# Six raw weight slots for the expert loop, two of them over the scan's rows, and gates as (tanh(x/2) + 1) / 2

## The chip, the cores and the metric

The kernel runs on one core of a Trainium2 chip (trn2). The metric is the device time of one execution in microseconds; the time before is 1294.22 us, the median of three runs (1288.75 to 1295.73). The engines are named as in the profile: PE is TensorE, DVE VectorE, ACT ScalarE, POOL GpSimd and SP SyncE, whose queue issues most of the weight loads.

## What is computed

Two layers of a backbone run over 128 context tokens and 128 latent tokens of width 1024, with one set of weights. Cut to what matters:

```python
# per layer, for each of the two streams
out = token_mixer(x * (1 + sc1) + sh1)
x = layer_norm(ALPHA * x + g1 * out)
ff = hier_moe(x * (1 + sc2) + sh2)
x = layer_norm(ALPHA * x + g2 * ff)

# token_mixer: three branches, then gates and one projection
gates = sigmoid(proj[..., OFF_GATE:N_IN].reshape(b, l, 3, D_MODEL))
merged = (gates[:, :, 0] * (y_att @ w_branch[0])
          + gates[:, :, 1] * (y_ssm @ w_branch[1])     # scan in two directions
          + gates[:, :, 2] * (y_gm @ w_branch[2]))
return merged @ w_o, k, v, h_fin

# hier_moe: 4 groups of 8 experts; a token takes one group and 2 of its experts
hid = silu(einsum('td,edf->tef', x, w1)) * einsum('td,edf->tef', x, w3)
y = einsum('tef,efd->td', hid * gates[:, :, None], w2)
```

## The kernel before

All weights are fp32. Each passes the core as a *piece* of 128 partitions by 2048 columns (1 MB) in four steps: a load into a slot of `raw`; ACT copies it into `wh` as fp32r, the high part; DVE subtracts the high part from the raw piece and gets the low part `wl`; PE multiplies with three products (high by high, high by low, low by high). There are 4 slots (`SLOTS`) and 3 pairs of parts (`PARTS`). A slot is free for the next load when DVE has subtracted (`part_low`), a pair of parts when PE has used both (`part_free`).

The mixer's pieces of a layer are listed in `PIECES`, those of the MoE in `BODY`: three for each of 32 experts, up (first half of the rows of w1 and w3), up (second half), and down. Every token is gathered by group, so an expert works on 128 rows. PE's order in the loop (`stream`) is: up of expert i, down of expert i - 1, transposition of the hidden rows of expert i. ACT takes the Silu (line 1772) between its conversions (line 1721), DVE the product with the gate (`hid`, line 2488) between its subtractions (line 1816, a helper for all its two-operand work). In the first group DVE also finishes the layer norm (experts 2 to 5, `x<-x,lnrow`). For each group but the first, POOL gathers the group's rows from memory (line 909, tile `grow`), and PE transposes them within experts 4 and 6 of the group before. After a group PE scatters its sum.

SyncE's queue takes the loads in their fixed order (`load`, line 732; `expert_loads`, lines 747 and 750). The first four pieces of a loop wait for the slots of the last mixer pieces, the last of which is the router's. Piece 4 waits for DVE's subtraction of piece 0, which follows the routing. Before piece 4 the queue also waits for the routing's decision, whether one round of the loop is enough (`need_ready`); it is, in these runs.

In the mixer, the scan of the state space branch runs in eight steps. In step n DVE forms the exponents `seg` (line 2291), ACT takes Exp of them (line 1692), for n of 4 and more also of the decay rows, `eb` (line 1689), DVE forms `W` (line 2313), and PE uses it in four small matmuls. Between the steps PE projects the gates of branches 2 and 1 (`SCAN_FILL`), one piece a step; ACT and DVE convert the pieces ahead. ACT evaluates the gates (`gate_take`, line 1605) after steps 2, 4 and 6 and after the last one, and before the scan for branch 0, just behind the Gelu of `gv`. `merge` multiplies them with the projected branches and adds; the merged rows are transposed and cut into high and low parts (`mT`, line 1708), and the output projection follows. Exp and Sigmoid alternate in the scan, and so do their tables, which ACT loads with ACT_TABLE_LOAD.

## Time and profile before

| | |
|---|---|
| median of 3 runs | 1294.22 us (1288.75 to 1295.73) |
| the profiled execution | 1292.93 us, of which the span of the profile is 1291.1 |
| PE busy | 1215.4 us, 94% of the span |
| DVE busy | 970.8 us, 75% |
| ACT busy | 740.6 us, 57% |
| POOL busy | 74.5 us, 6% |
| DMA | 358.83 MB, mean 278 GB/s |
| mean clock granted to PE | 0.966 |
| MoE loops, first to last Silu | 360.65 to 645.47 and 984.29 to 1266.54 us |
| scans, layer 0 and 1 | about 225 to 285 and 853 to 913 us |

Times in the views are microseconds from the span's start. A row of the timeline or of the groups names line, engine and operation, then output <- inputs with their shapes; behind it in brackets stands the idle time just before and the instruction that ended it. Busy time of PE counts matmuls that overlap in its pipeline, so a busy PE isn't at its peak. The clock is a share of full speed.

### The profile page before, as it was taken

Reading aid. Unit: us, or ns where it says so; the run is one execution under the profiler, and the core shown is the slowest. Engines: PE = TensorE matmul, PEld = TensorE weight load, DVE = VectorE, ACT = ScalarE, POOL = GpSimd, SP = SyncE. Lnnn points to the kernel's source line nnn. Section 1 sums busy time; section 2 is a strip of 40 time slices with the busy share of each in tenths; the row PEclk is TensorE's granted clock in tenths of the full one; section 3 lists DMA queues with packets and bytes.
Section 4 is the critical chain, followed back from the end, with each engine's and each line's share of the span. In section 5 each row is a group of like instructions: output and inputs, shape, how many; then the busy total and the mean of one; then the engine's idle time right before and its main releaser. Section 6 shows DMA issues by size and latency. Waiting matters only on the chain.

```text
span 1291.1 us, 15762 instructions
## 1 busy us (share of the span) xinstructions
PE 1215.4 (94%) x5950; PEld 950.3 (74%) x5953; DVE 970.8 (75%) x1159; ACT 740.6 (57%) x700; POOL 74.5 (6%) x121
## 2 busy tenths in 40 slices
PE   5999999999999999999979999998998999999994
PEld 1667777777677788887857777877777778788883
DVE  1645657787589889888878375768968988988887
ACT  1543553753467677677753255546437776777773
POOL 0401000101000000000020000010000000000000
PEclk8899998989999999999999999988999999999997
DMA  9978864636879999999976777445347999999991
GB/s 355 301 269 305 301 209 140 192 112 260 331 272 355 378 361 340 354 353 348 364 213 234 274 256 273 164 138 184 135 164 256 362 373 352 353 345 364 349 357 65
DMA packets 99491, 358.83 MB, mean 278 GB/s; under 512 B 9188, under 2 KB 12736, under 8 KB 83024
## 3 DMA queue, kind: packets, MB, share of 16 engines
q1 hardware_dynamic: 87504, 295.12, 63.2%
q0 software_dynamic: 11904, 62.63, 14.1%
q8 instruction: 49, 0.80, 0.2%
q14 instruction: 34, 0.28, 0.1%
HBM read 352.92 MB, written 5.83 MB: 278 GB/s over the span
## 4 chain that ended last, share of the span: by engine, by line
PE 65%; DVE 15%; DMA 8%; ACT 6%; issue 3%; DVEq 2%; ACTq 1%; SPq 1%; POOL 0%; POOLq 0%
PE bank L940 61%; DVE wl L1816 7%; DMA raw<-in_moe_w 5%; PE bank L943 4%; ACT wh L1721 2%; ACT wh L1511 2%; DMA first<-in_w_ada 1%; DMA adaw<-in_w_ada 1%; DVE tmp L1816 1%; DMA decay<-decay_rows 1%; DVE seg L2291 1%; ACTq L1606 0%; DVE xbc L2085 0%; DVE xbc L2082 0%; DVE x L1816 0%
## 5 line engine op out<-in xcount | busy, mean ns | idle before, releaser
L1816 DVE TENSOR_TENSOR wl<-raw,wh 128x2048 fp32r<-128x2048 f32 (+1 forms) x268 | 607.6, 2275 | 126.7 <-ACT wh L1511 67.0
L1721 ACT ACTIVATE wh<-raw 128x2048 fp32r<-128x2048 f32 x192 | 367.7, 1916 | 63.8 <-PE bank L940 28.4
L940 PE MATMUL bank<-wh,xgh 128*128 128x512 f32 x512 | 210.1, 410 | 0.0
L940 PE MATMUL bank<-wh,xgl 128*128 128x512 f32 x512 | 203.6, 398 | 0.0
L1511 ACT ACTIVATE wh<-raw 128x2048 fp32r<-128x2048 f32 (+1 forms) x76 | 142.3, 1872 | 100.2 <-PE bank L940 57.5
L940 PE MATMUL bank<-wh,hTh 128*128 128x512 f32 x448 | 186.2, 416 | 4.4 <-DVE wl L1816 2.5
L940 PE MATMUL bank<-wl,hTh 128*128 128x512 f32 x448 | 182.4, 407 | 0.0
L940 PE MATMUL bank<-wh,hTl 128*128 128x512 f32 x448 | 181.8, 406 | 0.0
L940 PE MATMUL bank<-wl,xgh 128*128 128x512 f32 x512 | 140.3, 395 | 0.0
L940 PEld LDWEIGHTS bank<-wl,xgh 128*128 128x128 f32 x512 | 96.1, 188 | 23.5 <-DVE wl L1816 0.2
L940 PEld LDWEIGHTS bank<-wh,xgl 128*128 128x128 f32 x512 | 97.1, 190 | 20.2
L940 PEld LDWEIGHTS bank<-wh,xgh 128*128 128x128 f32 x512 | 97.4, 190 | 19.6
L940 PEld LDWEIGHTS bank<-wh,hTh 128*128 128x128 f32 x448 | 87.8, 196 | 27.9 <-DVE wl L1816 4.9
L940 PEld LDWEIGHTS bank<-wh,hTl 128*128 128x128 f32 x448 | 87.3, 195 | 21.5
L940 PEld LDWEIGHTS bank<-wl,hTh 128*128 128x128 f32 x448 | 87.5, 195 | 19.5
L940 PE MATMUL bank<-wh,hTTh 128*128 128x512 f32 x256 | 101.3, 396 | 0.0
L940 PE MATMUL bank<-wh,hTTl 128*128 128x512 f32 x256 | 101.2, 395 | 0.0
L940 PE MATMUL bank<-wl,hTTh 128*128 128x512 f32 x256 | 80.7, 396 | 0.5 <-DVE wl L1816 0.4
L1778 ACT ACTIVATE hTTh<-bank 128x256 fp32r<-128x256 f32 x64 | 24.6, 384 | 66.5 <-PE bank L943 63.8
L940 PEld LDWEIGHTS bank<-wl,hTTh 128*128 128x128 f32 x256 | 47.9, 188 | 12.9 <-DVE wl L1816 1.4
L940 PEld LDWEIGHTS bank<-wh,hTTh 128*128 128x128 f32 x256 | 48.1, 188 | 11.8 <-issue 0.3
L940 PEld LDWEIGHTS bank<-wh,hTTl 128*128 128x128 f32 x256 | 48.1, 188 | 11.5
(303 smaller groups left out, 1480.1 us busy)
## 6 DMA issues: line engine op xcount, KB each, us to landing
raw<-in_moe_w SPq DMA_DIRECT2D x256, 512.0 KB, 5.2
raw<-in_moe_w SPq DMA_DIRECT2D x64, 1024.0 KB, 7.2
raw<-in_w_in SPq DMA_DIRECT2D x52, 1024.0 KB, 5.6
adaw<-in_w_ada POOLq DMA_DIRECT2D x32, 1024.0 KB, 5.7
raw<-in_w_branch SPq DMA_DIRECT2D x12, 1024.0 KB, 5.3
raw<-in_w_ada SPq DMA_DIRECT2D x8, 1024.0 KB, 9.9
raw<-in_w_o SPq DMA_DIRECT2D x8, 1024.0 KB, 4.9
first<-in_w_ada SPq DMA_DIRECT2D x4, 1024.0 KB, 16.7
```

The costliest lines, as they stand in the source:

```text
L940: return behind(nc.tensor.matmul(*args, **kw))
L943: return behind(nc.tensor.transpose(*args))
L1511: A_(wh[c][:, 0:n], raw[:, r, 0:n], ACT.Copy).then_inc(part_high[c], 1)
L1721: tally(A_(wh[c][:, :], raw[:, r, :], ACT.Copy), part_high[c])
L1778: tally(A_(hTTh[i == NE - 1][:, :, :], bank[TURN_BANK][:, 0:FF].rearrange("p (c t) -> p c t", c=2), ACT.Copy), hidT_high)
L1816: return V.tensor_tensor(o, a, b, op)
L2291: ins = V.tensor_scalar(seg[:, n % 2, i, :], decay[n % 2][:, i, :], acs[:, s, 8 * r + h:8 * r + h + 1], 0.0, ALU.subtract, ALU.min)
```

## The change

**The ring.** The expert loop takes its raw pieces from six slots instead of four. Slots 4 and 5 lie in a region `scan_rows` of 21 KB a partition, which holds in the mixer `rows3`, `wsT`, `h0`, `h0T`, `xbc` and `btok`; these are dead once the scan's branch is done and the new state is stored. So the first use of slot 4 in each layer waits for `y_ready[1]` and for `stored`. A piece of the loop now waits for the piece six before it, and at the loop's end the next layer's first four pieces wait for pieces 90 to 93 instead of 92 to 95. Conversion and subtraction find their slot modulo `RING`. The number of part pairs stays 3.

**The gates.** sigmoid(x) = (tanh(x/2) + 1) / 2. ACT evaluates Tanh with a scale of 0.5; the product in `merge` becomes (t + 1) * branch in one instruction; the factor 1/2 is applied where the merged rows are read from the transposition, on ACT as the scale of the copy and on DVE inside the subtraction.

The diff, with the renumbering of semaphore counts left out:

```diff
@@ -38,6 +38,7 @@
 SLOTS = 4
+RING = 6
 PIECE = 2048
@@ -92,15 +93,15 @@
-def slot_count(pieces, k):
-
-    return sum(incs(pieces[i]) for i in range(k % SLOTS, k + 1, SLOTS))
-
-
-LOAD_A = [[slot_count(p, k) for k in range(len(p))] for p in PIECES]
-LOAD_B = [slot_count(BODY, k) for k in range(len(BODY))]
-FULL_A = [a[-SLOTS:] for a in LOAD_A]
-FULL_B = LOAD_B[-SLOTS:]
+def slot_count(pieces, k, slots):
+
+    return sum(incs(pieces[i]) for i in range(k % slots, k + 1, slots))
+
+
+LOAD_A = [[slot_count(p, k, SLOTS) for k in range(len(p))] for p in PIECES]
+LOAD_B = [slot_count(BODY, k, RING) for k in range(len(BODY))]
+FULL_A = [a[-SLOTS:] + [0] * (RING - SLOTS) for a in LOAD_A]
+FULL_B = LOAD_B[-RING:]
 RAW_AT = [[p.index(key) for key in SPLIT] for p in PIECES]
@@ -364,13 +365,6 @@
         hrow = sb("hrow", [P, 40])
-        rows3 = sb("rows3", [P, 3, NW])
-        wsT = sb("wsT", [P, 4, P])
-        h0 = sb("h0", [HD, 2, HEADS, HD])
-        stout = h0
-        h0T = sb("h0T", [P, HEADS, HD])
-        xbc = sb("xbc", [P, 6, 2 * P])
-        btok = sb("btok", [P, 2 * P])
         tmp = sb("tmp", [P, D])
@@ -401,6 +395,18 @@
             return [nc.alloc_sbuf_tensor_at(n, shape, dt, offset=start + o * 1024) for n, shape, dt, o in tensors]
+
+        rows3, wsT, h0, h0T, xbc, btok, raw4, raw5 = region(
+            "scan_rows", 21,
+            ("rows3", [P, 3, NW], F32, 0),
+            ("wsT", [P, 4, P], F32, 6),
+            ("h0", [HD, 2, HEADS, HD], F32, 8),
+            ("h0T", [P, HEADS, HD], F32, 12),
+            ("xbc", [P, 6, 2 * P], F32, 14),
+            ("btok", [P, 2 * P], F32, 20),
+            ("raw4", [P, PIECE], F32, 0), ("raw5", [P, PIECE], F32, 8))
+        stout = h0
+        slot = [raw[:, i, :] for i in range(SLOTS)] + [raw4[:, :], raw5[:, :]]
@@ -734,20 +740,24 @@
                     kind, e, *h = BODY[i]
-                    s = i % SLOTS
-                    if i >= SLOTS:
-                        body_emptied(l, rnd, i - SLOTS)
+                    s = i % RING
+                    if i >= RING:
+                        body_emptied(l, rnd, i - RING)
                     elif rnd:
-                        body_emptied(l, 0, len(BODY) - SLOTS + i)
-                    else:
+                        body_emptied(l, 0, len(BODY) - RING + i)
+                    elif i < SLOTS:
                         slot_emptied(l, len(PIECES[l]) - SLOTS + i)
+                    elif i == SLOTS:
+                        sp.wait_ge(y_ready[1], l + 1)
+                        sp.sem_inc(sp_waited, 1)
+                        sp.wait_ge(stored, 48 * (l + 1))
                     if kind == "up":
...
                             src = A[w][l, e].rearrange("(p c) f -> p (c f)", c=DC)
-                            sp.dma_start(raw[:, s, n * 1024:(n + 1) * 1024],
+                            sp.dma_start(slot[s][:, n * 1024:(n + 1) * 1024],
                                          src[:, h[0] * 1024:(h[0] + 1) * 1024]).then_inc(slot_full[s], 16)
                     else:
-                        sp.dma_start(raw[:, s, :], A["moe_w2"][l, e].rearrange("(p c) n -> p (c n)", c=2)).then_inc(slot_full[s], 16)
+                        sp.dma_start(slot[s], A["moe_w2"][l, e].rearrange("(p c) n -> p (c n)", c=2)).then_inc(slot_full[s], 16)
@@ -765,22 +775,22 @@
                     load(l, i)
-                expert_loads(l, 0, 0, SLOTS)
+                expert_loads(l, 0, 0, RING)
                 sp.wait_ge(need_ready, l + 1)
...
                 with sp.If(more < 1):
-                    expert_loads(l, 0, SLOTS, len(BODY))
-                    for i in range(SLOTS):
-                        body_emptied(l, 0, len(BODY) - SLOTS + i)
+                    expert_loads(l, 0, RING, len(BODY))
+                    for i in range(RING):
+                        body_emptied(l, 0, len(BODY) - RING + i)
                         sp.sem_inc(slot_full[i], FULL_B[i])
-                        if l < L - 1:
+                        if l < L - 1 and i < SLOTS:
                             load(l + 1, i)
                 with sp.Else():
-                    expert_loads(l, 0, SLOTS, len(BODY))
+                    expert_loads(l, 0, RING, len(BODY))
                     expert_loads(l, 1, 0, len(BODY))
                     for i in range(SLOTS if l < L - 1 else 0):
-                        body_emptied(l, 1, len(BODY) - SLOTS + i)
+                        body_emptied(l, 1, len(BODY) - RING + i)
                         load(l + 1, i)
@@ -1602,7 +1612,7 @@
                         t = bank_full(act, l, name)
-                        frees(A_(dst[:, s, n * 512:(n + 1) * 512], t[:, :], ACT.Sigmoid), name)
+                        frees(A_(dst[:, s, n * 512:(n + 1) * 512], t[:, :], ACT.Tanh, scale=0.5), name)
                         act.drain().then_inc(gate_ready, 1)
@@ -1706,7 +1716,7 @@
                         A_(hTh[:, 4 * h:4 * h + 4, s * P:(s + 1) * P], t[:, :].rearrange("p (c t) -> p c t", c=4),
-                           ACT.Copy).then_inc(turned_high, 1)
+                           ACT.Copy, scale=0.5).then_inc(turned_high, 1)
                 ahead(("wo", 3))
@@ -1715,10 +1725,10 @@
                 def convert(tally, rnd, j):
-                    r, c = j % SLOTS, j % PARTS
+                    r, c = j % RING, j % PARTS
                     act.wait_ge(slot_full[r], N_LOAD[r].moe(l, rnd, LOAD_B[j]))
                     act.wait_ge(part_free[c], N_PART[c].moe(l, rnd, j // PARTS + 1))
-                    tally(A_(wh[c][:, :], raw[:, r, :], ACT.Copy), part_high[c])
+                    tally(A_(wh[c][:, :], slot[r], ACT.Copy), part_high[c])
@@ -1918,11 +1928,14 @@
-                def turned(b, name, high, low):
-
-                    t = bank[USE[l][name][0]]
+                def turned(b, name, high, low, scale=None):
+
+                    t = bank[USE[l][name][0]][:, :].rearrange("p (c t) -> p c t", c=4)
                     dve.wait_ge(turned_high, l * 10 + b + 1)
-                    frees(tt(low, t[:, :].rearrange("p (c t) -> p c t", c=4), high.bitcast(F32), ALU.subtract), name)
+                    if scale is None:
+                        frees(tt(low, t, high.bitcast(F32), ALU.subtract), name)
+                    else:
+                        frees(V.scalar_tensor_tensor(out=low, in0=t, scalar=scale, in1=high.bitcast(F32), op0=ALU.mult, op1=ALU.subtract), name)
@@ -2145,19 +2158,23 @@
                     gates_ = gate1 if b == 1 else gate
+
+                    def gated(out, t, s, hs):
+                        return V.scalar_tensor_tensor(out=out, in0=gates_[:, s, hs], scalar=1.0, in1=t[:, :], op0=ALU.add, op1=ALU.mult)
+
                     for h in range(2):
...
                                 t = bank_full(dve, l, f"br{b}{h}{s}")
-                                frees(tt(tmp[:, s * 512:(s + 1) * 512], t[:, :], gates_[:, s, hs], ALU.mult), f"br{b}{h}{s}")
+                                frees(gated(tmp[:, s * 512:(s + 1) * 512], t, s, hs), f"br{b}{h}{s}")
                                 drain()
...
                             out = merged[:, s, hs] if b == 0 else tmp[:, s * 512:(s + 1) * 512]
-                            frees(tt(out, t[:, :], gates_[:, s, hs], ALU.mult), f"br{b}{h}{s}")
+                            frees(gated(out, t, s, hs), f"br{b}{h}{s}")
                         if b:
@@ -2336,12 +2353,12 @@
                         part = (slice(None), slice(4 * h, 4 * h + 4), slice(s * P, (s + 1) * P))
-                        turned(6 + 2 * s + h, f"mT{s}{h}", hTh[part], hTl[part])
+                        turned(6 + 2 * s + h, f"mT{s}{h}", hTh[part], hTl[part], 0.5)
                 ahead(("wo", 3))
                 def lower(tally, rnd, j):
-                    r, c = j % SLOTS, j % PARTS
+                    r, c = j % RING, j % PARTS
                     dve.wait_ge(part_high[c], N_PART[c].moe(l, rnd, j // PARTS + 1))
-                    tally(tt(wl[c][:, :], raw[:, r, :], wh[c][:, :].bitcast(F32), ALU.subtract), part_low[c])
+                    tally(tt(wl[c][:, :], slot[r], wh[c][:, :].bitcast(F32), ALU.subtract), part_low[c])
...
                 rows("x2T", 1)
```

## Rows read from the trace of the kernel before

**Rows 1.** Table of stretches, one group of eight experts each: us, busy time of each engine, PE clock, DMA share, GB/s
```profile
370.88:445.41 74.53, 72.15 (x319) 56.85 (x318) 69.10 (x56) 52.68 (x44) 1.61 (x2) 1.00 0.97 363
...
518.29:591.74 73.45, 73.05 (x327) 58.72 (x326) 63.45 (x48) 52.68 (x45) 0.96 (x1) 1.00 0.95 349
...
992.24:1067.34 75.10, 72.25 (x319) 56.85 (x318) 69.53 (x56) 53.03 (x45) 1.60 (x2) 1.00 0.98 365
...
1140.30:1212.81 72.51, 72.51 (x327) 58.92 (x326) 63.71 (x48) 52.55 (x45) 0.97 (x1) 1.00 0.97 356
```

**Rows 2.** Timeline of ACT, line 1772 in layer 0: start, length, idle before
```profile
591.74 0.39 ACT L1772 ACTIVATE sil<-bank 128x256 f32<-128x256 f32 x1 [0.16 <-PE bank L940]
602.22 0.39 ACT L1772 ACTIVATE sil<-bank 128x256 f32<-128x256 f32 x1 [0.59 <-PE bank L940]
610.86 0.39 ACT L1772 ACTIVATE sil<-bank 128x256 f32<-128x256 f32 x1 [0.59 <-PE bank L940]
```

**Rows 3.** Waits, 345:680, then 950:1291: total us, times, longest
```profile
ACT wh L1721 <- DMA raw<-in_moe_w: 15.6, 21, 2.5
```
```profile
ACT wh L1721 <- DMA raw<-in_moe_w: 10.4, 12, 2.0
```

**Rows 4.** Chain of work in layer 0's loop: start, us, what
```profile
382.73 8.51 DMA raw<-in_moe_w
391.26 1.93 ACT wh L1721
393.21 2.29 DVE wl L1816
```

**Rows 5.** Timeline of PE in the scan, last step of layer 0, step 4 of layer 1
```profile
278.35 0.69 PE L940 MATMUL bank<-xs,W 128*128 128x64 f32 x2 [2.08 <-DVE W L1816]
```
```profile
888.80 0.56 PE L940 MATMUL bank<-xs,W 128*128 128x64 f32 x2 [3.06 <-DVE W L1816]
```

**Rows 6.** Timeline of SyncE's queue, then table of stretches, at the loops' start
```profile
351.44 0.33 SPq L750 DMA_DIRECT2D raw<-in_moe_w  x1
```
```profile
350.00:370.00 20.00, 18.73 (x93) 16.29 (x93) 15.48 (x40) 11.64 (x12) 0.00 (x0) 0.84 0.65 239
...
980.00:990.00 10.00, 8.73 (x43) 7.02 (x42) 7.49 (x20) 7.02 (x7) 0.00 (x0) 1.00 0.39 136
```

**Rows 7.** Timelines of ACT and of DVE at expert 1 of layer 0
```profile
370.88 0.39 ACT L1772 ACTIVATE sil<-bank 128x256 f32<-128x256 f32 x1 [0.59 <-PE bank L940]
```
```profile
373.98 0.48 DVE L2488 SCALAR_TENSOR_TENSOR hid<-bank,gg,sil 128x256 f32<-128x256 f32 x1
```

**Rows 8.** Groups of instructions on ACT: count, busy us, mean ns, idle before
```profile
L1605 ACT ACT_TABLE_LOAD x10 | 12.8, 1283 | 0.2
```

**Rows 9.** Chain of work in the scans of layer 0 and layer 1
```profile
249.98 1.30 ACTq L1606
...
252.75 1.28 ACT L1689
```
```profile
869.83 1.28 ACT L1692
...
882.45 1.28 ACT L1689
```

**Rows 10.** Table of stretches, end of the scan of layer 0
```profile
280.00:285.00 5.00, 5.00 (x14) 3.99 (x14) 4.00 (x9) 1.52 (x3) 0.00 (x0) 0.53 0.19 77
```

**Rows 11.** Groups of instructions on DVE, 350:680, by line
```profile
L2488 DVE SCALAR_TENSOR_TENSOR hid<-bank,gg,sil 128x256 f32<-128x256 f32 x32 | 15.3, 478 | 0.4
L1816 DVE TENSOR_TENSOR hTTl<-bank,hTTh 128x256 fp32r<-128x256 f32 x32 | 13.4, 418 | 3.0 <-ACT hTTh L1778 3.0
```

**Rows 12.** The tile grow, then timelines of GpSimd and PE
```profile
DMA to landing us min/median/max: 6.4/7.5/8.0
```
```profile
383.32 1.01 POOL L909 DMA_INDIRECT grow<-token_rows,slot_row  x1 [34.27 <-DVE slot_row L2466]
```
```profile
395.90 0.66 PE L943 MATMUL bank<-cst,grow 128*128 128x128 f32 x4
```

More of the change, by code:

```diff
@@ L86 @@
     assert len(_p) % SLOTS == 0 and [p for p in _p if p[0] not in RAW_KINDS] == SPLIT
-assert len(BODY) % SLOTS == 0 and len(BODY) % PARTS == 0
+assert len(BODY) % RING == 0 and len(BODY) % PARTS == 0
 ROUNDS = 2
@@ L121, in moe @@
         return self.base[l] + self.a[l] + rnd * self.b + n
-N_LOAD = [Loop([FULL_A[l][i] for l in range(L)], FULL_B[i]) for i in range(SLOTS)]
+N_LOAD = [Loop([FULL_A[l][i] for l in range(L)], FULL_B[i]) for i in range(RING)]
 RAW_FREED = [[sum(p[i][0] in RAW_KINDS for i in range(k % SLOTS, k + 1, SLOTS)) for k in range(len(p))] for p in PIECES]
@@ L477, in hybrid_backbone @@
             at += n
-        slot_full = [sem(f"slot_full{i}") for i in range(SLOTS)]
+        slot_full = [sem(f"slot_full{i}") for i in range(RING)]
         slot_free = [sem(f"slot_free{i}") for i in range(SLOTS)]
```

## The prediction

> **What bounds the kernel now.** I read the table of stretches first, cut at the starts of one group of experts, because TensorE (PE) is busy 94% of the span and an average hides where it waits. An undisturbed group of eight experts takes 72.51 us, the last of [rows 1]. [rows 2] give the beat inside it: 8.64 us from expert to expert, and 10.48 where a scatter lies between, so a scatter costs 1.84. The first group of a layer has no scatter and should take 72.51 - 1.84 = 70.67 us. It takes 74.53 and 75.10 in [rows 1], which is 3.86 and 4.43 too long, and the third group of layer 0 is 0.94 too long. I take the rest of the MoE loops as PE at its own pace.
>
> The waits name the cause of part of this: ScalarE (ACT) waits 15.6 and 10.4 us for raw weights in the two loops [rows 3]. In the chain of work [rows 4] one turn of a slot is visible: 8.51 us for the load, 1.93 to convert, 2.29 to subtract, after which the slot takes its next load. That is 12.7 us, over 4 slots 3.2 us a piece or 9.5 us an expert, more than the 8.64 that PE needs. The loop's start is bound by the latency of a ring too short. It isn't bound by it alone: the group moves 363 GB/s at a DMA share of 0.97 and VectorE (DVE) is busy 69.10 of its 74.53 us [rows 1].
>
> The second place is the scan of the mixer. There the chain runs through ACT and DVE, and PE waits for the matrix W before its small matmuls: 3.06 us in layer 1 and 2.08 us at the last step in layer 0 [rows 5].
>
> **The ring: what is moved.** Two more slots add no transfer; pieces 4 and 5 of each loop are issued earlier. In the old order piece 4 waits for the first subtraction and is issued at 351.44 [rows 6]. In the new one SyncE's queue issues slots 4 and 5 right behind slot 3. The two waits put ahead of slot 4 (the branch rows ready, the state stored) concern work of the scan, over some 50 us earlier, so nothing behind them in the queue, the wait for the routing's decision among it, is held up. Is there room on the DMA engines? In 350 to 370 us their share is 0.65 and in 980 to 990 it is 0.39 [rows 6], so 7.0 and 6.1 us of a full set of engines lie idle. Two pieces are 2.10 MB; at the 363 GB/s of [rows 1] they take 5.8 us and fit. The loop thus starts its steady part with 5.8 us of lead, and each later load is issued two turns earlier, which takes the 12.7 us turn to 12.7 / 6 = 2.1 us a piece. The latency is gone as a limit.
>
> What is late next? DVE. [rows 7] show expert 1 of layer 0: its first product is read at 370.88, and DVE, which has run without a gap, only writes the hidden rows from 373.98 to 374.46. PE fills the time with one down projection (12 of the 36 matmuls of an 8.64 us beat, 2.9 us), so it waits some 0.7 us, and a little more through the refill behind it. This doesn't depend on the ring. The lower bound of what stays in a first group is this 0.7 us; the upper one is the DVE time itself: 69.10 us busy and about 2.5 of gaps, 71.6 to 73 us for the group. I take 71.9, 1.2 above PE's own pace, nearer the first end because the DVE row already contains that stall. The first groups then give 74.53 - 71.9 = 2.6 and 75.10 - 71.9 = 3.2 us, and the third of layer 0 its 0.94: **6.7 us**. The shorter first group must draw part of its 27 MB (363 x 74.53) from the lead, 2.6 us x 363 GB/s = 0.9 MB of the 2.1, so the lead suffices. Bounds: 3 us (DVE keeps the first groups at 73 and above) and 9.2 (all of 3.86 + 4.43 + 0.94). The first loads of the next layer go out two pieces earlier too; PE has its own work there, so I give them 0, and less than 0.5 either way.
>
> **The gates: what is removed.** Tanh stands in for Sigmoid at line 1605. [rows 8]: a table load is 1283 ns and ten of them precede a gate. All ten go if Tanh is in the tables that Exp and Gelu use, and with them the reloads for Exp behind the gates in the scan; the ten alone are 12.8 us of ACT, but most of it lies beside PE's work. What counts is the loads on the chain [rows 9]. In layer 0 there is one pair, 249.98 and 252.75, 2.58 us together, just ahead of the exponential that DVE waits for; the pair of gate (2,0) there is covered, since PE runs on without a gap until W of step 4. In layer 1 the first W is later and the chain holds two pairs, the reloads at 869.83 and 882.45 and as many loads ahead of the gates, 5.1 us. The two exponentials and gates between them stay.
>
> What follows behind these is DVE's own chain, busy almost throughout, so it shifts by what ACT gives. In layer 0 the last W matmul stands at 278.35 and moves by 2.5; the lower bound is 2.1 (no more than PE's own wait there goes), the other 3.7, if the earlier ACT work also lets DVE run ahead before step 4 (half of the pair that was covered). In layer 1 the shift is at most 5.1. PE, however, runs at 0.53 of its clock in 280 to 285 after its waits at the end of layer 0's scan [rows 10], the lower of the two levels (1.2 of 2.4 GHz). After the change the W of the last two steps is what PE waits for in layer 1 too, so part of the gain can be given back there. I take 4.0 for layer 1, between 2.5 and 5.1. **The scan gives 6.5 us**, bounds 4.6 and 8.8. The Trainium skill ("ScalarE: Activation LUTs", "Table sets: the hidden batching unit") puts tanh into the set of exp, and sigmoid into another; by that rule the reloads of the scan vanish. The same page ("What ACT_TABLE_LOAD costs") adds a drain of 1380 ns to each switch, by which three pairs would be 16 us; the trace disagrees, as the chain gives the switch at 249.98 1.30 us in all, and the sum keeps that.
>
> The other edits: the gate product becomes a scalar_tensor_tensor on DVE (24 times), the four subtractions of a layer behind the merge too, and the copy of ACT gets a factor. The nearest rows are the 256-column pair of the loop [rows 11], 478 ns against 418. At 60 ns each, 32 operations are 1.9 us at most, nearly all beside matmuls, and some in the DVE chain ahead of the output projection. I take 0.3 us lost, between 0 and 1.9.
>
> **Sum.** 6.7 + 6.5 - 0.3 = 12.9 us. The profiled execution took 1292.93 us (span 1291.1 and 1.8 around it), so it would become 1280.0. It stands 1.3 us below the median 1294.22 of the runs shown, and so the median becomes **1281.3 us**.
>
> **Rivals.** (a) *The clock takes it back.* A stretch like 280 to 285 at 0.53 of the clock loses 5 x 0.47 = 2.4 us. If PE's new waits bring one more such stretch in each layer, 4.8 us go: 1286. For it: W of steps 6 and 7 comes out 1 to 3 us after PE wants it. Against it: the stretch may lie where PE has slack anyway, and layer 0 has one already. (b) *The loop stays bound by DVE and bandwidth.* The first groups keep 74 us or more; the ring gives 1 us and the scan 6.5: 1287. For it: DVE at 93% and DMA at 0.97. Against: 26.0 us of ACT waits for loads [rows 3] that DVE doesn't explain. (c) *Tanh doesn't share the tables*, the switches stay: the ring alone, 1287.5. (d) *More than forecast*: DVE gets ahead in both places, 9.2 + 8.8 = 18.0: 1276. (e) *Slower: the gathers.* The deeper ring keeps more raw loads in flight while GpSimd gathers the rows of the next group. [rows 12]: a gather issued at 383.32 lands 7.5 us later, at 390.8, and PE turns its rows at 395.90, 5.1 us of slack. Two more pieces served ahead would make it 13.3 us, only 0.7 us of wait, six times over: 4 us, not enough. To end 0.5% slower the six gathers must eat 12.9 + 6.5 = 19.4 us, 3.2 each, so they must land after 5.1 + 3.2 + 7.5 = 15.8 us: 1301. It decides only from twice the present time. The Trainium skill ("DMA: Bandwidth & Descriptors", "Queues, rings and completion order") has each DMA engine take turns between queues packet by packet, by which a gather in GpSimd's queue isn't behind SyncE's loads at all; no row here shows it.
>
> **Chances and range.** Forecast 0.62, (a) 0.12, (b) 0.12, (c) 0.05, (d) 0.06, (e) 0.03. About 0.5% (6.5 us) is what this measurement can tell from no change. Faster by more: the forecast, (d), nearly all of (a), two thirds of (b): 0.86. Within 0.5%: 0.11. Slower: 0.03. The range goes from the case (d) with the 3 us by which single runs of before differ, 1273, to (b) and (c) with 1.5 us above, 1289.
>
> **What would show it.** Right: no table load at 1605, 1689 or 1692; W waits of PE shifted from step 4 to steps 6 and 7; first groups near 72 us; ACT's wait for raw loads in the loops below 5 us. The ring is wrong if the first groups stay at 74 us with these waits gone (DVE or bandwidth), or if the waits stay. The gates are wrong if the step from the first W matmul to the last stays as long. A gather that lands after 13 us, or half clock in 860 to 920, would break the sum.

## The result and the profile after

| | before | after |
|---|---|---|
| median | 1293.09 us (1288.75 to 1298.76, 7 runs) | 1278.48 us (1276.04 to 1283.68, 7 runs) |
| ratio | | 0.9905 (0.9881 to 0.993), 9 to 15 us |
| the profiled execution | 1292.93 us, span 1291.1 | 1282.84 us, span 1281.0 |
| ACT instructions | 700 | 684 |
| loops, first to last Silu | 284.82 and 282.25 us | 281.19 and 279.14 us |

The change is faster, by about 1%, and the median lies 2.8 us below the forecast of 1281.3. The profiled execution is one of the slower of the kernel after. I split the 10.1 us between the two profiles by milestones: the first `W` matmul of a scan, the first one of its last step (called the last W below), and the first and the last Silu of a loop, each read in the timelines of PE and ACT:

| stretch, us | before | after | difference |
|---|---|---|---|
| start to first W, layer 0 | 232.33 | 234.81 | +2.5 |
| first to last W, layer 0 | 46.02 | 43.20 | -2.8 |
| last W to first Silu | 82.30 | 79.32 | -3.0 |
| loop, layer 0 | 284.82 | 281.19 | -3.6 |
| last Silu to first W, layer 1 | 214.39 | 213.71 | -0.7 |
| first to last W, layer 1 | 48.20 | 44.36 | -3.8 |
| last W to first Silu | 76.23 | 80.74 | +4.5 |
| loop, layer 1 | 282.25 | 279.14 | -3.1 |
| last Silu to the end | 24.56 | 24.53 | 0 |

The scans and the loops are where the change acts: 6.6 and 6.7 us. The rest moves by itself, up to 4.5 us in one stretch, and has to be told apart from it.

The table of stretches after, as in [rows 1] (us, busy time of PE, weight loads, DVE, ACT and GpSimd, PE clock, DMA share, GB/s): the first group of experts of each layer, the second of layer 0, the end of the scan and the loop's start as in [rows 10] and [rows 6], and the routing of layer 1.

```profile
366.12:439.76 73.64, 71.49 (x319) 57.02 (x318) 70.36 (x57) 52.44 (x45) 1.61 (x2) 1.00 0.99 375
985.27:1057.68 72.41, 71.46 (x319) 56.97 (x318) 69.27 (x56) 52.44 (x44) 1.59 (x2) 1.00 1.00 383
439.76:512.27 72.51, 72.51 (x327) 58.92 (x326) 64.19 (x51) 52.43 (x44) 0.99 (x1) 1.00 0.97 355
280.00:285.00 5.00, 4.78 (x21) 3.52 (x19) 4.26 (x9) 0.20 (x1) 0.00 (x0) 1.00 0.14 56
350.00:370.00 20.00, 16.51 (x82) 13.24 (x81) 16.61 (x35) 12.39 (x11) 0.00 (x0) 1.00 0.92 346
960.00:965.00 5.00, 3.95 (x20) 3.86 (x18) 1.76 (x11) 4.04 (x6) 0.71 (x1) 0.50 0.94 303
965.00:970.00 5.00, 4.14 (x19) 4.17 (x20) 3.90 (x11) 1.60 (x3) 0.00 (x0) 0.50 0.98 364
```

All groups but the first are at 72.51 to 72.54 us. The idle DMA time at the loop's start is used: a share of 0.92 where [rows 6] had 0.65. Half clock stood at the end of layer 0's scan before [rows 10] and isn't there now; it stands at the routing of layer 1 instead.

The waits after, in both loops. ACT's wait for raw weights [rows 3] is in neither list; what is left there is DVE waiting for the conversion:

```profile
DVE wl L1826 <- ACT wh L1731: 23.7, 51, 1.4
```

PE's waits for W, as in [rows 5]: steps 6 and 7 of layer 0, steps 4, 6 and 7 of layer 1.

```profile
273.84 0.43 PE L950 MATMUL bank<-xs,W 128*128 128x64 f32 x2 [1.68 <-DVE W L1826]
278.01 0.43 PE L950 MATMUL bank<-xs,W 128*128 128x64 f32 x2 [2.08 <-DVE W L1826]
877.32 0.41 PE L950 MATMUL bank<-xs,W 128*128 128x64 f32 x2 [0.51 <-DVE W L1826]
892.42 0.43 PE L950 MATMUL bank<-xs,W 128*128 128x64 f32 x2 [1.86 <-DVE W L1826]
896.59 0.43 PE L950 MATMUL bank<-xs,W 128*128 128x64 f32 x2 [2.07 <-DVE W L1826]
```

The wait of 3.06 us at step 4 of layer 1 has become 0.51. Step 4 of layer 0 has no wait any more; before, it had this one, which [rows 5] don't show:

```profile
259.09 0.41 PE L940 MATMUL bank<-xs,W 128*128 128x64 f32 x2 [2.40 <-DVE W L1816]
```

The chain in the scan no longer runs through ACT: there is no table load at the gates [rows 8] nor at the two exponentials.

Expert 1 of layer 0, as in [rows 7]: first PE, then DVE.

```profile
368.61 0.74 PE L950 MATMUL bank<-wl,hTTh 128*128 128x512 f32 x2 [1.59 <-DVE wl L1826]
371.29 0.48 PE L953 MATMUL bank<-cst,hid 128*128 128x128 f32 x2 [0.56 <-DVE hid L2505]
```
```profile
366.26 4.49 DVE L1826 TENSOR_TENSOR wl<-raw,wh 128x2048 fp32r<-128x2048 f32 x2
370.67 0.48 DVE L2505 SCALAR_TENSOR_TENSOR hid<-bank,gg,sil 128x256 f32<-128x256 f32 x1
```

DVE is busy without a gap from 359.34 to 373.68, and PE waits 2.15 us for it, at a low part and at the hidden rows.

### The profile page after: what moved, and what is told of

It is laid out like the page before. It is cut to its first block, busy times and chain, and to the rows that moved or that the text cites. A ratio compares the mean times of both kernels' runs of the same rounds, so it can differ in the third digit from the quotient of the medians.

```text
span 1281.0 us, 15755 instructions
## 1 busy us (share of the span) xinstructions
PE 1208.1 (94%) x5953; PEld 949.2 (74%) x5953; DVE 971.0 (76%) x1159; ACT 716.9 (56%) x684; POOL 74.5 (6%) x121
## 3 DMA queue, kind: packets, MB, share of 16 engines
q0 software_dynamic: 11904, 62.63, 13.9%
## 4 chain that ended last, share of the span: by engine, by line
PE 73%; DVE 11%; DMA 5%; ACT 4%; issue 2%; DVEq 2%; ACTq 1%; SPq 1%; POOL 0%; POOLq 0%
PE bank L950 69%; PE bank L953 4%; DVE wl L1826 4%; ACT wh L1521 2%; DMA adaw<-in_w_ada 2%; DMA first<-in_w_ada 1%; DMA raw<-in_w_in 1%; DVE tmp L1826 1%; DVE seg L2308 1%; DVEq L2333 1%; DMA decay<-decay_rows 1%; DVE xbc L2098 0%; DVE xbc L2095 0%; SPq L763 0%; DVE gv L1826 0%
## 5 line engine op out<-in xcount | busy, mean ns | idle before, releaser
L950 PEld LDWEIGHTS bank<-wh,xgh 128*128 128x128 f32 x512 | 96.8, 189 | 20.2 <-DVE xgl L1826 0.8
L950 PEld LDWEIGHTS bank<-wh,xgl 128*128 128x128 f32 x512 | 96.5, 189 | 20.2
```

What stands on the lines that cost most here:

```text
L950: return behind(nc.tensor.matmul(*args, **kw))
```

## The experiments

The milestones in the texts below are read as in the table above.

### The gates alone

The kernel before with all edits of the gates, and four slots in the loop:

```diff
-                        frees(A_(dst[:, s, n * 512:(n + 1) * 512], t[:, :], ACT.Sigmoid), name)
+                        frees(A_(dst[:, s, n * 512:(n + 1) * 512], t[:, :], ACT.Tanh, scale=0.5), name)
```

> The gates alone, with four slots in the loop as before. My theory (the gates' table loads stand on the chain of the scan, the ring acts on the loop alone): 5 to 7 us faster than before; no table load at the gate or at the two exponentials; from the first scan matmul to the last W matmul 2.5 to 3 us less in layer 0 and 4 to 4.5 us less in layer 1; the W waits of step 4 gone and steps 6 and 7 at 1.7 to 2.1 us; the first groups of experts unchanged at 74.5 and 75.1 us with ScalarE's waits for raw weights between 10 and 16 us a loop. Rival, that the whole gain comes from the ring: within 1 us of before. Rival, that the clock at the end of the scan eats it: 2 to 3 us faster.

Measured: ratio 0.9943 (0.9913 to 0.9972) over 9 runs, 7.4 us faster, between 3.6 and 11.2. From the first to the last W 43.35 us in layer 0 and 44.09 in layer 1, that is 2.7 and 4.1 less than before. Both rivals fall. One expectation missed: the loops aren't unchanged but longer, 286.79 and 283.59 us, and the first groups took 77.63 and 76.85. ACT's waits for raw weights are there as expected, 12.4 and 12.9 us. The first group of layer 0, and a stretch within it:

```profile
364.65:442.28 77.63, 73.90 (x319) 57.98 (x318) 69.09 (x56) 52.76 (x44) 1.61 (x2) 0.98 0.94 351
420.00:425.00 5.00, 3.59 (x15) 2.27 (x13) 3.78 (x2) 3.42 (x3) 0.00 (x0) 1.00 1.02 410
425.00:430.00 5.00, 4.00 (x12) 3.25 (x13) 5.00 (x8) 2.86 (x3) 0.00 (x0) 0.66 0.98 347
```

In 420 to 425 the DMA engines are full and 410 GB/s arrive, yet each engine stands for a part of the time: ACT waits 1.60 us for a raw piece at 421.22, DVE 1.22 for ACT, and PE 1.86 for DVE's hidden rows at 426.00. In 425 to 430 the granted clock is 0.66. No profile with six slots has a wait of ACT for raw weights in its list; that four slots can't bridge such a stall is my reading of that.

### The ring alone

The kernel after with all edits of the gates taken back:

```diff
-                        frees(A_(dst[:, s, n * 512:(n + 1) * 512], t[:, :], ACT.Tanh, scale=0.5), name)
+                        frees(A_(dst[:, s, n * 512:(n + 1) * 512], t[:, :], ACT.Sigmoid), name)
```

> The ring of six slots alone, with Sigmoid and its table loads. My theory: 6 to 7 us faster than before (3.6 in the first loop, 3.1 in the second, and little elsewhere); the first groups near 73.6 and 72.4 us, all others at 72.5; no wait of ScalarE for raw weights in the loops; the scan as before. Rival, that DVE and not latency holds the loop's start: under 2 us faster, first groups at 74 or more. Together with the gates alone it should give the whole change, 12 to 14 us, if the two parts are independent.

Measured: ratio 0.9955 (0.9933 to 0.9977) over 12 runs, 5.8 us faster, between 3.0 and 8.7. The loops are 281.16 and 279.17 us, as after the whole change; the scans take 46.09 and 48.07 us, as before (PE waits 2.47 us for W at step 4 of layer 0). 7.4 and 5.8 make 13.2, the change 12.3 by its ratio: within their intervals the two parts add up.

### The kernel before once more

No edit.

> The kernel before once more, for a second profile. The kernel with the gates alone had loops of experts 2.0 and 1.3 us longer than the profiled execution of before, with the same four slots. If a ring of four slots makes the loops vary from execution to execution with the service of the loads, this one's loops differ from 284.8 and 282.3 us by 0.5 us or more, while with six slots every profile shows 281.2 and 279.1 within 0.1. If the gates themselves slow the loops, it shows 284.8 and 282.3 again.

Measured: 1292.39 us in one run; loops of 284.78 and 281.40, first groups of 75.31 and 74.51 (74.53 and 75.10 in [rows 1]). So with four slots the three profiles give for both loops together 567.1, 566.2 and 570.4 us, and with six the profiles of the change, the ring alone, the next kernel and the one with 64 bytes further down give 560.0 to 560.3. With six slots the gates don't slow the loops. With four it is less clear: the two profiles of the kernel before agree in the loop of layer 0 (284.82 and 284.78) and differ by 0.85 us in that of layer 1, where I had put the mark at 0.5, and the 570.4 us stand in one profile, the only one with the gates. That four slots lose another amount in each execution fits this; that the gates add to it there isn't excluded.

### Six slots without the lead

```diff
                         sp.wait_ge(stored, 48 * (l + 1))
+                    if not rnd and SLOTS <= i < RING:
+                        body_emptied(l, 0, i - SLOTS)
```

> The whole change, but the first loads of slots 4 and 5 wait for the subtractions of pieces 0 and 1, so that the loop has six slots without the lead of two pieces. If the latency of a slot's turn is what held the first groups, this keeps most of the gain: at most 1 us slower than the change, first groups at 73 to 74. If it is the lead that gives the gain (the loads are bound by bandwidth and the two pieces fill idle time of the DMA engines), the first groups return to 74.5 and 75 and it is 3 to 6 us slower than the change.

Measured: 1278.55 us, ratio 0.989 (0.9861 to 0.9919), the same as the change. Its first groups:

```profile
362.58:436.22 73.64, 71.50 (x319) 57.04 (x318) 70.36 (x57) 52.44 (x45) 1.61 (x2) 1.00 0.99 377
979.31:1051.71 72.40, 71.45 (x320) 57.29 (x320) 69.26 (x56) 52.45 (x45) 1.60 (x2) 1.00 0.99 384
```

Within 0.01 us the groups of the change. The early issue of pieces 4 and 5 isn't needed. But the run takes away less than its name says. In layer 0 pieces 4 and 5 are issued 14.3 and 13.9 us ahead of the first Silu after the change, and 8.3 and 3.9 us ahead of it here; pieces 6 and 7 wait for slots that are free by then, and follow at once. The 20 us that correspond to 350 to 370 after the change are these, with the DMA engines as busy as there:

```profile
346.47:366.47 20.00, 16.52 (x82) 13.25 (x81) 16.60 (x35) 12.40 (x11) 0.00 (x0) 1.00 0.93 329
```

So six slots fill the idle DMA time with or without the head start. Whether the loop needs the two more turns in flight or the transfers in that idle time, no run separates.

### One pair of table loads put back

The kernel after, with one activation on a spare tile, behind the gate of step 4 and, in a second kernel, of step 2:

```diff
+        probe = sb("probe", [P, 2])
...
                         gate_take(*((2, 0), (2, 1), (1, 0))[n // 2 - 1])
+                    if n == 4:
+                        A_(probe[:, 0:1], C["iota"][:, 0:1], ACT.Sigmoid)
```

> The change with one activation of two columns more (a Sigmoid on a spare tile) on ScalarE behind the gate of step 4, in both layers; it brings back exactly the pair of table loads that stood on the chain before. Theory (the pair costs what its two loads take, 2.57 us plus some 0.2 for the activation, less what PE's cover hides): a W wait of 2 to 2.7 us at step 4 in layer 0 where there is none, in layer 1 the wait there grows from 0.5 to some 3 us, and the last W matmul, counted from the first, comes 2.5 to 2.8 us later in each layer. Rival, that a switch also drains the engine and costs as much again: 5 us or more. Rival, that the gain in the scan had another cause: under 1 us.

> The same added pair of table loads, but behind the gate of step 2. Theory: in layer 0 PE has cover there (it reaches W of step 2 to 4 without a wait), so the last W matmul moves by less than 1 us; in layer 1, where the gate projections run further ahead of DVE by the row of step 4 (0.5 us of wait), it moves by 1.5 to 2.8 us. Rival, that every pair costs its 2.6 us wherever it stands: 2.5 or more in both layers.

ACT in the first kernel, layer 0, then PE at step 4 in both layers of the first kernel:

```profile
251.07 1.28 ACT L1710 ACT_TABLE_LOAD   x1
252.36 0.20 ACT L1710 ACTIVATE probe<-cst 128x1 f32<-128x1 f32 x1
252.57 1.28 ACT L1700 ACT_TABLE_LOAD   x1
```
```profile
258.90 0.41 PE L951 MATMUL bank<-xs,W 128*128 128x64 f32 x2 [1.87 <-DVE W L1829]
876.98 0.41 PE L951 MATMUL bank<-xs,W 128*128 128x64 f32 x2 [3.16 <-DVE W L1829]
```

The two kernels took 1275.22 and 1269.50 us, one run each. They must be set against a kernel with the same placement of the tiles (the one with 32 bytes, below, 1265.11 us). From the first W to that of step 4 it needs 24.21 and 25.13 us; the pair at step 4 makes this 25.82 and 28.03, at step 2 24.58 and 26.42. A pair of 2.76 us with its activation costs 1.6 and 2.9 us at step 4, 0.4 and 1.3 at step 2. A load is 1.28 us and no more (251.07 + 1.28 = 252.35, and the probe starts at 252.36), so the rival with a drain falls, and so does the one that every pair costs its full length. Layer 0 has more cover at step 4 than I had expected (2.5 to 2.8 us), and layer 1 a little more at step 2 (1.5 to 2.8). The four prices add up to 6.2 us; the scans gave 6.6. By layer they fit less well: 2.0 us where layer 0 gave 2.8, and 4.2 where layer 1 gave 3.8. The pairs at step 6 and behind the last step weren't put back.

### What holds the scan after the change

```diff
-                    if n == 6:
-                        scanned(0)
                 branch_turned(2)
+                scanned(0)
...
-                branch_rows(l, 1, z)
-                branch(l, 2, (1,))
+                branch(l, 2, (1,), lambda: branch_rows(l, 1, z))
```

The function given to `branch` is called behind its first stream.

> The change, and behind it one more: VectorE takes the finishing of the first stream's scan rows (five operations, 3.8 us, between steps 6 and 7) after the last W, and TensorE turns the branch rows between the two streams of the last branch 2 piece instead of ahead of it. My theory: after the change the scan is bound by VectorE's chain in steps 5 to 7, not by ScalarE; the waits of 1.7 and 2.1 us for W at steps 6 and 7 go in both layers and some 1.4 us of a wait for z come back, so 2 to 3 us a layer, 4 to 6 us faster than the change. Rival: VectorE's total is the bound, the wait only moves to the turning of z or to the merge, and it is within 1 us of the change.

Measured: 1276.9 us, ratio 0.9878 (0.9853 to 0.9903); 3.5 us less than the change by the ratios and 1.6 by the medians, but the intervals overlap, so a gain isn't shown. The profile tells what happened. The waits for W at steps 6 and 7 are gone, from 3.76 to nothing in layer 0 and from 3.93 to 0.31 in layer 1, and these stand in layer 0 instead (in layer 1 the wait for z is 1.95 us):

```profile
283.19 1.23 PE L953 MATMUL bank<-cst,z 128*128 128x128 f32 x8 [1.78 <-DVE z L2345]
294.23 0.51 PE L950 MATMUL bank<-wh,yTh 128*128 128x512 f32 x1 [1.12 <-DVE wl L1827]
```

So both theories held in part: the order made the waits for W, and behind it the wait moves to z, by DVE's total. The 4 to 6 us of my theory aren't shown. The next kernel shortens it, and takes DVE off the loop's second expert:

```diff
-                    tt(y.rearrange("t (h d) -> t h d", h=HEADS), xs[:, s, :].rearrange("t (h d) -> t h d", h=HEADS),
-                       bc(hrow[:, 32:40], 2, HD), ALU.mult)
...
-                    frees(tt(y, t[:, :], y, ALU.add), f"y{s}")
+                    frees(tt(y, t[:, :], rows3[:, s, :], ALU.add), f"y{s}")
...
-                    tt(tmp[:, NW:D], z[:, s, :], z[:, s, :], ALU.mult)
...
-                    V.tensor_reduce(small[:, s:s + 1], tmp[:, NW:D], X, ALU.add)
+                    V.bn_stats(stats[:, s, 0:6], z[:, s, :])
...
+                    if n in (2, 3):
+                        tt(rows3[:, n - 2, :].rearrange("t (h d) -> t h d", h=HEADS), xs[:, n - 2, :].rearrange("t (h d) -> t h d", h=HEADS),
+                           bc(hrow[:, 32:40], 2, HD), ALU.mult)
...
-                        if i == 0:
+                        if i == 1:
                             select(tally, rnd, 1)
```

> The reordered scan tail of the run before, with VectorE's work in it shortened: the product of xs and D is taken in steps 2 and 3, where VectorE waits for ScalarE's conversions, and the mean square comes from bn_stats and bn_aggr in place of a product and a reduction, 3.0 us less between the last W and z; and in the loop of experts the selection of the second group (0.8 us on VectorE) moves from expert 0 to expert 1. Theory, that VectorE's chain is what holds the scan's tail and the loop's second expert after the change: the waits for z (1.8 and 1.95 us) go, the time from the first expert's Silu to the last falls by 0.5 to 0.8 us in both layers, and the whole is 5 to 8 us faster than the change, near 1272. Rival, that the merge or the clock takes it up: within 2 us of the reordered tail, 1275 to 1277.

Measured: 1270.91 us (1266.61 to 1281.54, 6 runs; the profile is of the slowest), ratio 0.9811 (0.9785 to 0.9838), about 12 us below the change by the ratios, 7.6 by the medians. The waits for z are gone, and in each layer 0.83 us for a low part stays. Expert 1 to expert 2 takes 10.21 us in layer 1 instead of 10.76, the 0.55 forecast at its lower end. But loop 1 is longer, 283.00 us, which I hadn't expected. DVE at its expert 12:

```profile
1081.92 0.68 DVE L1827 TENSOR_TENSOR xgl<-bank,xgh 128x512 fp32r<-128x512 f32 x1
1085.62 0.48 DVE L2508 SCALAR_TENSOR_TENSOR hid<-bank,gg,sil 128x256 f32<-128x256 f32 x1 [3.01 <-issue]
```

Its Silu was done at 1081.22; DVE stands for 3.01 us with nothing in the profile that it waits for, and PE behind it for 2.65. The granted clock is then 0.76 in 1085 to 1090 and 0.90 in 1090 to 1095, some 1.7 us more, and the group takes 76.95 us where the change has 72.54. The last kernel below has the same gap at the same instruction (3.10 us), no other profile has it. I had thought of the loading of DVE's code, but the queues that bring instructions move six packets around this group (1060 to 1130), as many as in the same place after the change (1065 to 1135), where there is no gap. The cause stays open; there is no run with the shortened scan and without the moved selection.

### The placement of the tiles

Both kernels with the probe tile ran an expert in 8.48 us, which nothing in them should do. Three kernels, the change with nothing but an unused tile of 8, 16 or 24 columns (32, 64, 96 bytes a partition):

```diff
         hrow = sb("hrow", [P, 40])
+        sb("pad", [P, 8])
```

> The change with an unused tile of 32 bytes a partition behind hrow, nothing else. It moves the token, mixer, turned and context tiles from an address of 32 modulo 64 to a multiple of 64, as the two-column probe tile of the switch runs did by chance; in both of those the undisturbed beat of an expert was 8.48 us and the step of the scan 5.95, against 8.64 and 6.05 in every profile without it. If the placement of the tiles that the matmuls read does this, the beat is 8.48, an undisturbed group 71.2 to 71.4 us and the whole some 15 us below the change, 1262 to 1267. If the extra activation or the chip did it, 8.64 and 72.51 stay, and it is within 2 us of the change.

> The same with 64 bytes, so that everything moves, but the tiles stand at 32 modulo 64 again. If it is the address modulo 64, the beat is 8.64 and an undisturbed group 72.51 us, as in the change. If any shift does it (the distance to the weight parts), 8.48 and 71.2 to 71.4.

> The same with 96 bytes: the tiles stand at a multiple of 128. If only modulo 64 counts, the beat is 8.48 as with 32 bytes. If a larger alignment gives more, it is shorter, 8.3 or less.

One undisturbed group, the second of layer 0, with 32, 64 and 96 bytes (after the change it is 72.51, above):

```profile
438.53:509.88 71.35, 71.35 (x327) 58.94 (x326) 64.22 (x51) 52.44 (x45) 0.99 (x1) 1.00 0.98 363
```
```profile
442.96:515.42 72.46, 72.46 (x327) 58.87 (x326) 64.19 (x51) 52.50 (x44) 0.99 (x1) 1.00 0.98 356
```
```profile
438.01:509.03 71.02, 71.02 (x327) 58.92 (x326) 64.18 (x52) 52.34 (x45) 0.99 (x1) 1.00 0.98 364
```

The beat of an expert is 8.48, 8.64 and 8.44 us. A shift alone does nothing (64 bytes); a start of the tile regions at a multiple of 64 bytes takes 1.9% off the beat, and of 128 another 0.5%. On the chip the 32 bytes give 1265.11 us, ratio 0.9784 (0.9747 to 0.9821): 1.2% below the change, more than the change itself gave. The single runs with 64 and 96 bytes took 1283.95 and 1266.88 us, so that the 96 bytes beat the 32 is seen in the groups alone. The granted clock is 1.00 in all three rows. In the groups of instructions the matmuls differ and PE's own loads of its stationary side don't (with 64 and with 96 bytes, 445 to 505 us):

```profile
L951 PE MATMUL bank<-wh,xgl 128*128 128x512 f32 x55 | 21.7, 394 | 0.0
L951 PEld LDWEIGHTS bank<-wh,xgl 128*128 128x128 f32 x55 | 10.4, 188 | 2.0
```
```profile
L951 PE MATMUL bank<-wh,xgl 128*128 128x512 f32 x56 | 21.9, 391 | 0.0
L951 PEld LDWEIGHTS bank<-wh,xgl 128*128 128x128 f32 x56 | 10.5, 188 | 1.9
```

The weight parts lie ahead of the added tile and didn't move; slots 4 and 5 did, and so did the tokens, hidden rows and selections, from which PE loads its stationary side. Which of them matters, and how, stays open. Before and after the change the regions stand at 32 modulo 64, so it plays no part in the result.

### All together

The shortened scan with the 96 bytes.

> The shortened scan of e8_short_scan together with the 96 bytes of e11_pad96. If the two are independent: 1270.9 less the gain of the placement (8.44 for 8.64 us an expert is 12.8 us over 64 experts, and the same 2.3% of the mixer's matmuls some 10 more, of which the waits for VectorE take back a part; e9_pad32 gave 13.4 with 8.48), so 1253 to 1258. If DVE's chain becomes the bound as PE gets faster: 1258 to 1263, with waits for W and z of 1 us and more in the scans and first groups no shorter than 71.5 us.

Measured: 1254.62 us (1250.98 to 1257.88, 6 runs), ratio 0.9699 (0.9665 to 0.9732): by the ratios 39 us below the kernel before and 27 below the change. That is within the 1253 to 1258 of two independent gains. The first and second group of layer 0:

```profile
357.46:429.96 72.50, 70.67 (x319) 56.85 (x318) 70.27 (x59) 52.36 (x44) 1.61 (x2) 1.00 1.00 380
429.96:500.97 71.01, 71.01 (x327) 58.92 (x326) 64.24 (x52) 52.35 (x44) 0.99 (x1) 1.00 0.98 365
```

## Why the prediction was right, and where it wasn't

The forecast of 12.9 us lies in the measured 9 to 15, and both parts and both causes are borne out by a run of their own. Inside the parts several terms were off.

**The ring, 6.7 us.** The loops gave 3.63 + 3.11 = 6.7 us in the profiled pair, and the ring alone 5.8 on the chip. The cause was the one named: with the slots, ACT's waits for raw weights go. But the sum was right by two errors that cancel. From Silu 0 to Silu 9 layer 0 took 84.76 us before and 82.43 after, layer 1 83.05 and 80.35, so the start of the loop gave 2.3 and 2.7 us, not 2.6 and 3.2. The rest came from what the sum had left out: the second groups, 72.88 and 72.96 us before, also wait for loads and gave 0.4 each; the third of layer 0 gave its 0.94 as said.

DVE was named rightly as the next bound, and its term holds only with a slow expert ahead of it. Before, and with the ring alone, expert 0 of layer 0 takes 10.23 us at a granted clock of 0.83, and PE then waits 0.55 us at expert 1, near the 0.7 of the prediction; with the ring alone the group behind it is 72.14, near the 71.9. After the change expert 0 takes 8.79 us at a clock of 1.00, PE waits 2.15, and the group is 73.64. DVE starts on the hidden rows of expert 1 13.33 us after the first Silu before and 13.34 after. So what PE wins in expert 0 it waits for in expert 1, the edge of the first group is a poor cut, and the two experts from Silu 0 to Silu 2 take 20.7 us in all three. That is DVE's, and the kernel that took work off DVE moved it to 20.2 (the 32 bytes alone to 20.6).

**The lead, 5.8 us.** The step that failed is the one that counts the lead as a store, of which the first group draws 0.9 MB: with pieces 4 and 5 issued 5.9 and 10.0 us later the groups are the same. The 0.92 of the DMA engines in 350 to 370 isn't its mark either, since it is 0.93 without the head start. The other step, a turn of 12.7 us over six slots in place of four, is what is left. It fits all profiles, but isn't separated from the idle DMA time that six slots fill as well.

**The gates, 6.5 us.** 2.8 in layer 0 and 3.8 in layer 1, against 2.5 and 4.0. The added pairs give the terms one by one: 1.6 and 2.9 at step 4, 0.4 and 1.3 at step 2. In layer 0 the pair on the chain was thus not the whole 2.5 and the covered one not 0; their sum is 2.0, and the 0.8 that is missing isn't put down to a pair. The lower bound of 2.1 for layer 0 was taken from the wrong wait: the 2.08 us at the last step stand after the change as before, and what went is the 2.40 at step 4, which the prediction hadn't read.

**The other edits, 0.3 us.** Nothing is seen of it. The 60 ns of [rows 11] belong to another form: the scalar of that scalar_tensor_tensor is a column of a tile (`gg`), one value a partition, while the gates have the constant 1.0. With a constant the gates' instruction takes 683 ns at 512 columns, against 688 for the product before. At the same width, and with no input from a bank, it is 692 with a constant and 748 with a scalar from a tile. These are rows of after:

```profile
L2163 DVE SCALAR_TENSOR_TENSOR tmp<-gate,bank 128x512 f32<-128x512 f32 x16 | 10.6, 683 | 2.3 <-PE bank L950 2.0
L1985 DVE SCALAR_TENSOR_TENSOR x<-x,root,lnrow 128x512 f32<-128x512 f32 x4 | 2.8, 748 | 0.2
L2202 DVE SCALAR_TENSOR_TENSOR S<-bias,cst 128x512 f32<-128x512 f32 x4 | 2.8, 692 | 9.4 <-PE bank L950 9.0 <-issue 0.4
```

**Rival (a), the clock.** In this profile 4.5 us went back in layer 1, though for the most part not where I had looked. Part is at the end of the scan (0.82 to 0.84 in 895 to 905, which the prediction had named as a sign that would break the sum), the larger part at the routing: from the router's last matmuls to the end of the first selection of rows (`selg`) it took 955.64 to 971.45 us, 15.8, against 966.37 to 978.41, 12.0, before. The granted clock is 0.65 in 955 to 960 and 0.50, the lower of the two levels (1.2 of 2.4 GHz), in 960 to 970; this row of after is from there:

```profile
958.37 3.65 PE L953 MATMUL bank<-cst,merged 128*128 128x128 f32 x16
```

The same 16 transpositions took 1.94 us before. No run shows the change to be the cause. From the last Silu of layer 0 to the first of layer 1 the profiles without the new gates show 338.8 and 339.0 us (before, twice) and 343.2 (the ring alone), those with them 338.8 (the change), 338.4 (the gates alone) and 335.6 (without the lead), though this last one has the same PE and ACT code there as the change. The ring alone has the half clock at the routing too, the kernel without the lead hasn't. So where half clock falls moves this stretch by 3.2 and 4.4 us between kernels with the same code in it; what decides it stays open, and the two profiles of the kernel before agree. In layer 0 the same thing was a gain of 3 us (last W to first Silu, no stretch below 1.00 at the end of the scan) that I had at nothing. The profiled 1282.84 us lies above the 1280.0 forecast and the median below its own; these 4.5 us are a part of that, not shown to be the whole.

**Rival (b)**, DVE and bandwidth: true of the second expert, not of the loop. The first groups now move 375 and 383 GB/s at a share of 0.99 to 1.00, so little is left there. **Rival (c)**: refuted; the loads right behind the Gelu of `gv` (180.14 and 807.43 before) went too. **Rival (d)**, 18.0 us: outside the measured 9 to 15. **Rival (e)**, the gathers: they now land in

```profile
DMA to landing us min/median/max: 6.5/7.7/9.2
```

The longest is 1.2 us longer than in [rows 12]; PE turns the first one's rows at 392.37, 12.35 us after its issue at 380.02, so at least 3.1 us are left, and no wait for them appears.

## What to carry to other kernels

Latency per turn over the number of slots, set against the time that PE needs for a piece, told here that a ring was too short. Two more slots were enough, and a head start on top of them added nothing. Look at more than one profile of before: with four slots the two loops together took 566.2 to 570.4 us, with six 560.0 to 560.3. An activation whose table differs from its neighbours' cost its two loads in full only where ACT was on the chain, and the way to know is to put a single pair back. A price must be read from a row of the same form: a constant scalar and one from a tile differ by 56 ns here. After a gain, follow the wait that took its place by one engine and one instruction: here an order, 3 us of DVE work and a moved selection were together worth about as much as the change.

## What the runs showed of the hardware that I had not expected

- The start address of the tiles that PE reads counts: regions at 32 modulo 64 bytes gave 8.64 us an expert, at 64 modulo 128 8.48, at a multiple of 128 8.44, with the same instructions at full clock; 1265.11 against 1278.48 us on the whole.
- DVE can stand 3.0 and 3.1 us at one instruction, the same in two kernels, with nothing in the profile to wait for: the two kernels with the shortened scan, in which a selection had moved by one expert, far ahead of that place.
- PE's half clock falls in other stretches between kernels with the same code there: the stretch of 338.8 us after the change is 335.6 without the lead.
- A scalar_tensor_tensor on DVE with its scalar from a tile takes 748 ns at 512 columns, with a constant 692.
